# The modulation product in four-column-strip float32 matmuls spread over the first layer, and a pair attention three steps deep

## What is computed

```python
def first_block(x, c, ctx, c_ctx, mod_w, mod_b, ...):
    silu_c, silu_cc = silu(c), silu(c_ctx)            # two vectors of 1024
    for l in range(2):
        # mod_w[l] is 1024 x 6144: shift, scale, gate of the mixer; shift, scale, gate of the feed-forward
        sh_a, sc_a, g_a, sh_f, sc_f, g_f = split(silu_c @ mod_w[l] + mod_b[l], 6)
        csh_a, csc_a, cg_a, csh_f, csc_f, cg_f = split(silu_cc @ mod_w[l] + mod_b[l], 6)
        a_lat = rms_norm(h_lat) * (1 + sc_a) + sh_a    # the context likewise with csh_a, csc_a
        o_lat, o_ctx = mixer_l(a_lat, a_ctx)           # layer 0: 8 MLA and 8 neighbourhood heads; layer 1: 16 windowed heads
        h_lat = h_lat + g_a * o_lat
        h_lat = h_lat + g_f * swiglu(rms_norm(h_lat) * (1 + sc_f) + sh_f)
        # the context likewise, in layer 0 only
    return rms_norm(h_lat, final_norm)
```

## Time and profile before

| | us |
|---|---|
| median of 3 runs | 3670.92 (3665.43 to 3671.42) |
| the profiled execution | 3665.97 |
| its span, first to last instruction | 3664.7 |
| PE busy in the span | 3314.5 |
| DVE / ACT / POOL busy | 2223.3 / 1768.6 / 225.0 |
| mean granted clock of PE | 0.942 of full |

### The profile page before, as it was taken

One profiled execution on the slowest core, in us unless ns is written; L12 is line 12 of the kernel. 1 busy time (PEld: TensorE's weight loads), 2 busy tenths in 40 slices (PEclk: granted clock), 3 DMA queues, 4 the chain that ended last, 5 costly groups with the idle time before them and its releaser, 6 DMA issues.

```text
span 3664.7 us, 52201 instructions
## 1 busy us (share of the span) xinstructions
PE 3314.5 (90%) x19560; PEld 2812.7 (77%) x19560; DVE 2223.3 (61%) x4465; ACT 1768.6 (48%) x3736; POOL 225.0 (6%) x290
## 2 busy tenths in 40 slices
PE   7799899999889977898699999997789869999999
PEld 3375578877569976797578999987589758999998
DVE  6733543333666565568966666667457886666665
ACT  6732433322345433532955555553442395555554
POOL 0001200000110035000000000004400000000000
PEclk9988989998889977799999999998789999999999
DMA  8830022332215622343055666662134305566564
GB/s 310 301 106 24 13 69 92 92 90 71 64 59 184 200 76 59 93 150 121 1 162 186 187 184 184 185 208 96 42 113 146 104 1 184 184 186 188 184 186 153
DMA packets 134932, 479.99 MB, mean 131 GB/s; under 512 B 15385, under 2 KB 17305, under 8 KB 133913
## 3 DMA queue, kind: packets, MB, share of 16 engines
q1 hardware_dynamic: 132080, 467.59, 40.5%
q10 hardware_dynamic: 2600, 9.04, 0.7%
HBM read 475.53 MB, written 1.05 MB: 130 GB/s over the span
## 4 chain that ended last, share of the span: by engine, by line
PE 81%; DVE 9%; issue 3%; ACT 3%; DMA 3%; ACTq 0%; DVEq 0%
PE psum L646 14%; PE psum L648 14%; PE psum L647 14%; PE psum L2252 7%; PE psum L2253 7%; PE psum L2254 7%; PE psum L2174 6%; PE psum L2098 4%; PE psum L507 3%; DMA raw<-in_mod_w 3%; DVE w_lo L229 2%; PE psum L915 1%; PE psum L519 1%; DVE conv_part L1383 1%; ACT prob L1021 1%
## 5 line engine op out<-in xcount | busy, mean ns | idle before, releaser
L229 DVE TENSOR_TENSOR w_lo<-raw,w_hi 128x512 fp32r<-128x512 f32 x1664 | 1133.5, 698 | 795.8 <-ACT w_hi L220 766.8
L220 ACT ACTIVATE w_hi<-raw 128x512 fp32r<-128x512 f32 x1664 | 1010.6, 626 | 869.2 <-PE psum L648 658.9
L646 PE MATMUL psum<-x_hi,w_hi 128*128 128x256 f32 x2096 | 600.3, 286 | 34.5 <-DVE w_lo L229 27.3
L648 PE MATMUL psum<-x_hi,w_lo 128*128 128x256 f32 x2096 | 597.0, 285 | 0.0
L647 PE MATMUL psum<-x_lo,w_hi 128*128 128x256 f32 x2096 | 596.6, 285 | 0.0
L646 PEld LDWEIGHTS psum<-x_hi,w_hi 128*128 128x128 f32 x2096 | 401.4, 192 | 47.2 <-DVE w_lo L229 29.7
L2252 PE MATMUL psum<-w_hi,wt_hi 128*128 128x512 f32 x1024 | 406.5, 397 | 6.5 <-DVE wt_lo L2310 6.5
L647 PEld LDWEIGHTS psum<-x_lo,w_hi 128*128 128x128 f32 x2096 | 401.2, 191 | 7.9
L2253 PE MATMUL psum<-w_lo,wt_hi 128*128 128x512 f32 x1024 | 406.6, 397 | 0.0
L2254 PE MATMUL psum<-w_hi,wt_lo 128*128 128x512 f32 x1024 | 405.4, 396 | 0.0
L648 PEld LDWEIGHTS psum<-x_hi,w_lo 128*128 128x128 f32 x2096 | 400.3, 191 | 0.0
(11 more groups left out here) (324 smaller groups left out, 4867.8 us busy)
## 6 DMA issues: line engine op xcount, KB each, us to landing
raw<-in_v SPq DMA_DIRECT2D x256, 512.0 KB, 4.2
raw<-in_u SPq DMA_DIRECT2D x190, 512.0 KB, 3.5
raw<-in_mod_w SPq DMA_DIRECT2D x96, 512.0 KB, 4.8
raw<-in_w_gate_up SPq DMA_DIRECT2D x88, 512.0 KB, 3.5
u_raw<-in_u SPq DMA_DIRECT2D x66, 512.0 KB, 3.5
raw<-in_w_in SPq DMA_DIRECT2D x40, 512.0 KB, 3.7
raw<-in_w_down SPq DMA_DIRECT2D x32, 512.0 KB, 3.5
raw<-in_w_peer SPq DMA_DIRECT2D x32, 512.0 KB, 3.7
```

Of the source, the lines that this page charges most:

```text
L220: self.nc.scalar.activation(self.hi[:, m % 4, :], self.half(m), ACT.Copy).then_inc(self.rounded[m % 4], 1)
L229: self.nc.vector.tensor_tensor(self.lo[:, m % 4, :], self.half(m), self.hi[:, m % 4, :], ALU.subtract).then_inc(self.ready[m % 4], 1)
L646: pe.matmul(out[:, 0:width], hi[:, w], x_hi, start=(c == 0), stop=False)
L648: mm = pe.matmul(out[:, 0:width], lo[:, w], x_hi, start=False, stop=(c == total - 1))
```

## The change

**Modulation.** `mod_w` is laid out anew: 6 groups of 2048 columns, 8 steps (chunks of 128 rows) a group, two whole units a step, 48 steps. A whole unit (`load_whole`, `take_whole`) isn't rounded by ACT and DVE; PE reads it from the ring's slot as float32, and the slot is free when PE has used it. One step is four float32 matmuls of 128 x 32 by 128 x 512, with outputs on partitions 0, 32, 64 and 96 of bank 4; the stationary side holds the two vectors and 30 columns of zeros. A group is closed by one `fill` of 128 x 512, one `turn` of four matmuls with `pick_rows` into bank 5, and one `add`. The additions of 1 are made to the bias once.

**Where its steps stand.** Group 0 (layer 0's mixer shift and scale) is made at the start: steps 0 to 2, then one of steps 3 to 7 behind each of the first five chunks of the first norm's column sums. The steps of group 1 follow one each on the projection's tiles 0 to 7, those of group 2 on the tiles 0 to 6 of layer 0's output product (two on tile 0), groups 3, 4 and most of 5 one on each of layer 0's 22 feed-forward rounds, the last two on down tiles 0 and 1. Both `Modulate` of layer 0 and the first of layer 1 wait for the groups that they read.

**Lookahead and transfers.** `ahead` is 2 in place of 3 from layer 0's start to the end of its output product. The loads of `mla` constants move from ACT's queue to SP's behind the load of projection tile 9; the load of `na_table` moves to SP's behind the value weights.

**Attention.** PE starts with three scores, and its order is turn(s), score(s+3), values(s-1). Maxima of both heads are one reduce over both banks and biases of both heads one addition; in the windowed attention the bias covers only the 128 keys of the other tile. ACT makes both copies of the turned weights. DVE's order is maxima(s+3), invert(s+2), finish(s-1). In `MixAttention` DVE's order becomes combine(s+1), maxima(s+3), invert(s+2).

```diff
 class Ring:
-    def load(self, src, name=None):
...
-        if u >= NSLOT:
-            m = 2 * (u - NSLOT) + 1
-            self.nc.sync.wait_ge(self.ready[m % 4], m // 4 + 1)
+    def begin(self, src):
+        u = len(self.slot_free)
+        if u >= NSLOT:
+            self.nc.sync.wait_ge(*self.slot_free[u - NSLOT])
...
+    def load_whole(self, src):
+        u = self.begin(src)
+        self.whole.append(u)
+        self.slot_free.append((self.used, len(self.whole)))
...
-        while self.scalar_made < min(self.scalar_seen + AHEAD, 2 * self.units):
+        while self.scalar_made < min(self.scalar_seen + self.ahead, len(self.halves)):
...
 class Modulation:
+    def tensor(self, step):
+        k, pe, (g, c) = self.k, self.k.nc.tensor, divmod(step, DC)
...
+        units = [k.ring.take_whole() for _ in range(2)]
+        for b in range(4):
+            m = pe.matmul(use.tensor[32 * b:32 * b + 32, :], self.silu[:, c, :],
+                          units[b // 2][:, (b % 2) * 512:(b % 2 + 1) * 512], start=(c == 0), stop=(c == DC - 1))
+            if b % 2:
+                m.then_inc(k.ring.used, 1)
...
+    def fill(self, g):
+        act.wait_ge(self.k.ring.used, 2 * DC * (g + 1))
...
+        act.activation(self.row(g)[:], use.tensor[:], ACT.Copy).then_inc(use.read.sem, 1)
...
 class EvenMixer(ModulationSteps):
+        super().__init__(mod, 1, {n: (DC + n,) for n in range(DC)}, 8, 9, 10)
...
     def sync(self):
+        for c in range(DC):
+            if c == DC - 1:
+                self.proj.sync_first()
+            self.mod.sync(c)
+        self.proj.sync_rest()
...
     def tensor(self):
-        self.modulated.tensor()
+        for c in range(3):
+            self.mod.tensor(c)
+        hold(pe, self.x_done)
+        self.modulated.tensor_sums(lambda c: self.mod.tensor(3 + c) if c < 5 else None)
+        self.mod.turn(0)
+        self.modulated.tensor_spread()
...
     def scalar(self):
+        k.ring.ahead = 2
+        self.modulated.scalar_rms(self.x_done)
+        k.ring.round(0)
+        self.mod.fill(0)
+        self.modulated.scalar_apply([self.mod.done(0)])
...
 class PairAttention:
     def tensor(self):
-            if s + 2 < n:
-                self.score(s + 2)
             self.turn(s)
+            if s + 3 < n:
+                self.score(s + 3)
...
     def vector(self):
+            if s + 3 < n:
+                self.maxima(s + 3)
             if s + 2 < n:
-                self.maxima(s + 2)
-            self.copy_vector(s)
+                self.invert(s + 2)
...
 class Ffn:
     def tensor(self):
+            if self.mod is not None:
+                self.mod.tensor(24 + f)
+            if self.mod is not None and f in (9, 17):
+                self.mod.turn(3 + f // 16)
```

More of the change, by code:

```diff
@@ L270, with __init__ @@
 class Setup:
[L271 to L274, removed]
+    def __init__(self, k, silu):
+        self.k, self.silu = k, silu
+        self.made = k.named("constants_made").take(3)
+        self.done = [self.made.after(3)]
     def vector(self):
@@ L279, in vector @@
         nc.vector.memset(k.eps, EPS).then_inc(self.made.sem, 1)
+        nc.vector.memset(self.silu[:], 0.0).then_inc(self.made.sem, 1)
 class Modulation:
-    BLOCKS = 24
     def __init__(self, k):
         self.k = k
[L289 to L294, removed]
-        self.fetch = Fetch(k, "c", (self.cT[:], k.io["cT"]), (self.modb[:], k.io["mod_b"]),
[L296 to L317, removed]
-            pe.wait_ge(*use.free())
[L319 to L325, removed]
@@ new lines, in __init__, with reserve, row, done @@
+        self.silu_made = k.named("c_silu").take(1)
+        self.bias_made = k.named("scale_bias_made").take(1)
+        self.rows, self.cols = [], []
+    def reserve(self, groups):
+        for _ in range(groups):
+            self.rows.append(self.k.bank[4].use(written=0))
+            self.cols.append(self.k.bank[5].use())
+    def row(self, g):
+        return self.row_places[g // 2 > 0]
+    def done(self, g):
+        return self.cols[g].emptied()
+    def sync(self, step):
+        for half in range(2):
+            self.k.ring.load_whole(self.k.io["mod_w"][2 * step + half])
@@ L357, in fill @@
[L357 to L380, removed]
@@ L664, in sync, with sync_first, sync_rest @@
     def sync(self):
[L665 to L667 removed]
+        self.sync_first()
+        self.sync_rest()
+    def sync_first(self):
+        self.first_half = len(self.k.ring.halves)
+        load_tile(self.k, self.w, self.tiles[0], self.cuts)
+    def sync_rest(self):
+        for n, t in enumerate(self.tiles):
+            if n > 0:
+                load_tile(self.k, self.w, t, self.cuts)
+            if self.between is not None:
+                self.between.sync_between(n)
     def full(self, n):
@@ L732, in sync @@
     def sync(self):
-        self.first_half = 2 * self.k.ring.units
+        self.first_half = len(self.k.ring.halves)
         for t in range(DC):
             load_tile(self.k, self.w, t, self.cuts)
+            if self.between is not None:
+                self.between.sync_between(t)
     def full(self, n):
@@ L1662, in vector @@
         k, dve = self.k, self.k.nc.vector
-        self.modulated.vector(self.start)
+        k.ring.ahead = 2
+        self.modulated.vector_rms(self.x_done)
+        k.ring.remain(0)
+        self.mod.add(0)
+        self.modulated.vector_apply([self.mod.done(0)])
         self.proj.vector()
```

342 lines of the change are left out of this document (204 added, 138 removed).

## The result

The changed kernel took 3560.99 us (median; 3556.54 to 3564.15), the kernel before beside it 3670.67: a ratio of 0.9698, 95% interval 0.9685 to 0.9712. That is 109.7 us less. The forecast was 3555, with a range of 3532 to 3600.

The account below looks back on a forecast made before the run. PE was taken to bound the dense stages (81% of the wait chain), transfers the start; -150 + 46 + 6.5 + 3 + 4 - 6 - 16 + 0 = -112.5 from 3666.0 gave 3553.5, named as 3555, range 3532 to 3600.

Parts of the forecast that it names:

- Start: Beginning of layer 0: `a_scaled` starts at about 48.7 us in place of 199.0, -150 (bounds -156 and -143).
- The step: Dense stages: four matmuls overlap fully, 1.15 us a step (0.95 to 3.43), 40 steps, +46.
- the feed-forward: Layer 0's feed-forward: about 30 us longer, from 22 + 2 steps and three turns of 1.3 each.
- The rivals of partial packing and of none: Modulation steps: partial, 1.7 to 2.3 us each, about 3590, chance 0.16; none, 3.43 each, about 3654, chance 0.08.
- Projection: Layer 0's projection: tile and step take 6.98 us, the ring adds +3; 12 us longer in the profile after.
- the ring: Projection tiles 1 to 8: three units per tile in four slots, loads just arrive, +3 (0 to 10).
- Output product: Layer 0's output product: two steps behind tile 0 bring a stall of about 3.5 us; +4 (0 to 9).
- Slower rival: Ring: whole units make PE wait for landing and rounding at each of 40 steps, about 3790; chance 0.05.
- Layer 0's attention: First half gains nothing; second half's pair of steps falls from 6.05 to 5.2 us, -6 (0 to -9).
- Layer 1's attention: Steps fall from 4.89 to 3.5 us, 13 steady steps, less for the first: -16 (-5 to -22).
- The rest: `MixAttention`, where `invert` now stands behind `maxima`: 0 +- 3.
- From sum to median: Whole kernel: -112.5 against the profiled 3666.0 gives 3553.5; median of runs lies 5.0 above that execution; named 3555.

Follow-up runs that it names:

- the two runs that made them true: Changed kernel with each step's four matmuls on two strips, 3589.69 us, and on one strip, 3668.95 us; one execution each, modulation values wrong.
- the direct comparison: Changed kernel with the pair attention of the kernel before put back in both layers: 3585.67 us, 21.5 more than the changed kernel beside it.
- the two-strip kernel: Changed kernel with the four matmuls of a step alternating between two strips in place of four, modulation values wrong: 3589.69 us in one execution.

## Why the prediction was right, step by step

**Start: -150 forecast, -148.4 measured.** The order of events was right, and luck had a part in the size. I took the step at 1.15 us and the transfers as the pace; at the start a step takes 1.93 and PE sets the pace at 3.66 per step and chunk, which came out right only because the transfers would have needed nearly the same, 3.4. What is missing is one wait: step 7 ended at 39.6 and not at 37.5, after 1.96 of waiting for its second unit. I had counted the bytes of the projection's first unit and not the slot that it takes. Behind step 7 the terms were 11.2 forecast and 11.0 measured.

**The step: 1.15 forecast, 1.2 measured** in the dense stages. This was the term with the widest bounds, 0.95 to 3.43, and the extrapolation from its nearest row (L938, two strips) held. 22 rounds x 1.2 stand in the feed-forward's +28.9, where two steps and three turns more had me at 31.5. A round with a turn is 0.89 longer than its neighbours (13.28 against 12.39), where I took 1.3. The rivals of partial packing and of none are out by the two runs that made them true: 3590 and 3669, where I had put them at 3590 and 3654. The second was 15 short: 6 is the miss of the forecast itself, and the rest comes from 3.43 as the step's full price; with entering and leaving it is 3.75 (14.95 - 11.20).

The Trainium skill (TensorEngine Tiling (Array Packing), Key Properties) says that changing the tiling mode drains the engine. The trace agrees that the change has a price and bounds it: 0.2 us for entering and leaving together, whatever part of them is the drain. The Trainium skill (TensorEngine Tiling (Array Packing), Overview, Theoretical Speedup) gives up to 4 times where the small side is 32 or less; this case shows 3.62/1.06 = 3.4.

**Projection: +13.5 forecast (9.2 for steps, 1.3 for the turn, 3 for the ring), +13.4 measured,** with 2.9 us of ring waits, though in two places and not spread out. **Output product: +14.5 forecast, +17.0 measured.** The stall of 3.5 behind tile 0 was 4.23. The step that failed is what it leaves behind: I let a stall cost its own length. PE's clock was at 0.50 behind it, and the next tile took 2.9 us longer. The stall's price is 7 and not 4. Tile and step came to 6.79 where I had 6.98.

**Slower rival.** The ring exposes a load fully only where two steps stand together; elsewhere 0 to 2.3 us. The lookahead of 2 belongs to this. With 3, ACT would have to round the first half of output tile 1 ahead of the evictions before the attention; that load needs the slot of step 16, which PE reaches only after the attention. The waits would close a circle; this is argued from the order, and no run tried it.

**Layer 0's attention: -6 forecast, +4.6 measured (+1.6 from its first score to its last value matmul).** Here the reasoning was wrong. I counted ACT's work (4.4 of 6.05 us a pair), PE's, and POOL's chain, and saw nothing full. I did not follow the copies in ACT's order: they stand behind the exponentials of two steps later, so moving DVE's copy to ACT put the bank of the turned weights into the loop of the scores. Copies first, one exchange of order, took the pair from 6.24 to 5.40. The old period was misread as well: 6.05 is the shorter of two pairs that take turns, and their mean is 6.17. So the change left the pair nearly where it was: eight pairs at 0.07 are 0.5 of the 1.6 lost, and the rest stands where the second half begins and ends.

**Layer 1's attention: -16 forecast, -27.4 in the profiles, 22 in the direct comparison.** The period came out at 3.33 for 3.5, and the first steps gained too, which I had left out. Of the -27.4, 2.7 are not the attention's: the third norm's 64 column sums took 13.67 us in the profile before and 11.00 in this one, and 13.53 in the second profile of the changed kernel. Half of the bias is 0.27 us of every two steps; the rest is the third step in flight with one reduce in place of two, and which of these gave how much is open.

**The rest: 0 forecast, +10.0 in the first profile.** The mixer of the second block took 7 of them. The second profile of the same kernel has it 5 us shorter at a higher clock, and twelve profiles of changed kernels spread over 8 us (187.8 to 195.5), so the miss is of the size by which executions differ. But most of them lie near 193 and the one profile of before at 186.3; what part of the 7 belongs to the change stays open. The good total owes something to cancellation: attention 0 missed by +10.6, attention 1 by -11.4.

**From sum to median.** The sum, -112.5, was made against the profiled execution and missed its like there by 10.6 (-101.9); it is near the medians' -109.7 because that profile of before was a fast one. And 3553.5 with the 5.0 between this execution and the median is 3558.5; I named 3555, which is not what the working gives. 3558.5 would have been 2.5 from the measured 3561.

## What to carry to other kernels

A matrix-vector product whose weights are read once can lie in the gaps of the transfers of later dense stages, if its matmuls fill the array side by side on strips; cost it by the rounds with and without it, since entering and leaving is a sixth of its price. When work moves from an engine to another with free time, write down which instructions will stand ahead of it there and whether one of them waits for the loop that the moved work now serves: order, not load, decided here. A stall on PE is to be priced with the slow clock that follows it, here 2.9 us behind one of 4.23. And before a gain is put down to an edit, the stretches at the low clock want to be compared too: here they moved one stage by some 3 us between profiles.

## What was not expected of the hardware

- Float32 matmuls of 32 columns on four strips take 1.06 us together, on two 1.91 and on one 3.62: the array's price is that of the most loaded strip, and 0.2 us.
- In the first 50 us the profile's granted clock reads 1.00, yet a step takes 1.93 us where it takes 1.06 later, and a chunk of sums 1.8, as in the stretch of the earlier trace rows whose clock is 0.57. In the two-strip kernel, whose steps keep PE busy longer, a chunk takes 1.05 in the same stretch. The durations, not that number, tell which level held there.
- A gap of 4.23 us on PE was followed by 2.9 us of extra time for the next tile at clock 0.50.
- The granted clock over the same work differs between executions (0.85 and 0.95 over one projection), and one stage of some 190 us came out 5 us apart in two executions of the same kernel.
